# Order and queues of the first transfers, and what the warm-up multiplies, in a streamed two-block layer kernel

## The reference

```python
def first_block(x, norm1_g, w_in, ...):
    h = hybrid_layer(x, ...)
    return rmsnorm(h, final_g)

def hybrid_layer(x, layer, norm1_g, w_in, ...):
    xn = rmsnorm(x, norm1_g[layer])
    u = xn @ w_in[layer]                      # [256, 1024] @ [1024, 5632]
    q_sb, k_sb, v_sb, f_raw, i_hg, q_hg, g_hg, gate_sb, gate_hg = split(u)
    ...                                       # stick-breaking attention, HGRN2, gates, w_out
    h = x + merged @ w_out[layer]
    return h + square(relu(rmsnorm(h, norm2_g) @ w_ff1)) @ w_ff2

def second_block(x, ...):                     # two layers: gated linear attention, differential attention
    ...                                       # each followed by a SwiGLU block and a gate
```

## Time and profile before

| | us |
|---|---|
| three runs | 1041.59, 1041.59, 1043.47 (median 1041.59) |
| the profiled execution | 1042.02 |
| its span, first to last instruction | 1040.2 |

### The profile page before, as it was taken

The page is one execution under the profiler, slowest core; times in us unless marked ns, Lnnn a source line. Parts: engine busy times, 40 slices in busy tenths (PEclk is TensorE's granted clock), DMA queues, the critical chain, the costliest instruction groups (busy, mean ns, idle before and its releaser), DMA issues.

```text
span 1040.2 us, 15841 instructions
## 1 busy us (share of the span) xinstructions
PE 1033.5 (99%) x6394; PEld 911.2 (88%) x6394; DVE 729.4 (70%) x869; ACT 596.5 (57%) x752; POOL 57.4 (6%) x53
## 2 busy tenths in 40 slices
PE   8999999999999999999999999999999999999998
PEld 8998999888888889888888888889998888888887
DVE  6888887676565568965766666677989676666665
ACT  5777545553444457765644444476777664444464
POOL 0000001200000030002006000010000200000010
PEclk9999999999999999999999999999999999999999
DMA  8746353645546545355456555455524365465641
GB/s 297 235 170 199 123 200 130 214 166 196 208 162 207 198 143 202 124 184 177 162 201 209 184 186 201 163 191 174 163 82 163 132 203 202 164 207 185 211 164 41
DMA packets 129352, 185.33 MB, mean 178 GB/s; under 512 B 3328, under 2 KB 102912, under 8 KB 129280
## 3 DMA queue, kind: packets, MB, share of 16 engines
q1 hardware_dynamic: 128416, 183.27, 51.8%
q10 hardware_dynamic: 704, 0.53, 0.2%
q0 software_dynamic: 160, 0.52, 0.2%
HBM read 183.26 MB, written 1.05 MB: 177 GB/s over the span
## 4 chain that ended last, share of the span: by engine, by line
PE 97%; DVE 1%; DMA 1%; ACT 0%; issue 0%; ACTq 0%; DVEq 0%
PE PS L435 95%; PE PS L443 2%; DMA HS<-in_xt_dram 1%; DVE SC L2570 0%; DVE WL L1892 0%; ACT AR L1768 0%; DVE AR L2592 0%; ACT X L1314 0%; DVE HS L2619 0%; ACTq L426 0%; DVE O L2627 0%; DVE AR L2565 0%; DVE AR L2558 0%; ACT WH L1268 0%; ACT AR L1704 0%
## 5 line engine op out<-in xcount | busy, mean ns | idle before, releaser
L1885 DVE TENSOR_TENSOR WL<-RAW,WH 128x2048 fp32r<-128x2048 f32 (+3 forms) x174 | 371.1, 2139 | 107.1 <-ACT WH L1268 106.7
L1268 ACT ACTIVATE WH<-RAW 128x2048 fp32r<-128x2048 f32 (+3 forms) x183 | 327.8, 1794 | 80.6 <-PE PS L435 73.9
L435 PE MATMUL PS<-WH,X 128*128 128x512 f32 (+1 forms) x1104 | 302.7, 355 | 0.0
L435 PE MATMUL PS<-O,WH 128*128 128x512 f32 (+1 forms) x880 | 239.1, 361 | 0.0
L435 PEld LDWEIGHTS PS<-WH,X 128*128 128x128 f32 x1104 | 195.8, 189 | 29.8 <-issue 1.9
L435 PE MATMUL PS<-X,WH 128*128 128x256 f32 (+1 forms) x864 | 200.8, 331 | 1.9 <-ACT WH L1268 1.7
L435 PE MATMUL PS<-WL,X 128*128 128x512 f32 (+1 forms) x552 | 194.6, 353 | 0.0
L435 PEld LDWEIGHTS PS<-O,WL 128*128 128x128 f32 x744 | 134.4, 189 | 22.7
L435 PE MATMUL PS<-O,WL 128*128 128x256 f32 x744 | 153.2, 281 | 0.0
L435 PE MATMUL PS<-WH,O 128*128 128x512 f32 (+1 forms) x464 | 141.0, 378 | 0.1
L435 PEld LDWEIGHTS PS<-O,WH 128*128 128x128 f32 x880 | 137.6, 190 | 3.3 <-issue 0.3
(11 more groups left out here) (222 smaller groups left out, 778.4 us busy)
## 6 DMA issues: line engine op xcount, KB each, us to landing
RAW<-in_ffn_w_in_dram SPq DMA_DIRECT2D x44, 1024.0 KB, 5.0
RAW<-in_w_ff_dram SPq DMA_DIRECT2D x32, 1024.0 KB, 5.3
RAW<-in_ffn_w_out_dram SPq DMA_DIRECT2D x22, 1024.0 KB, 4.9
RAW<-in_w_in_dram SPq DMA_DIRECT2D x18, 1024.0 KB, 5.2
RAW<-in_gla_w_in_dram SPq DMA_DIRECT2D x12, 1024.0 KB, 5.3
RAW<-in_diff_w_in_dram SPq DMA_DIRECT2D x12, 1024.0 KB, 5.2
RAW<-in_ple_w_gate_dram SPq DMA_DIRECT2D x8, 1024.0 KB, 4.8
RAW<-in_w_out_dram SPq DMA_DIRECT2D x4, 1024.0 KB, 4.8
```

What stands on the lines that cost most here:

```text
L435: return e.matmul(o, l, r, start=start, stop=stop, skip_group_check=skip)
L1268: act(high, raw, ACT.Copy).then_inc(s["w_hi"], 1)
L1885: e.tensor_tensor(low, raw, high.bitcast(F32), ALU.subtract).then_inc(s["w_lo"], 1)
```

## The change

- ACT issues the norm weights first and then feature group 0; groups 1 and 2 are issued by SP, group 1 ahead of the joint piece of block 1, group 2 ahead of the pieces of blocks 2-3, group 3 ahead of those of blocks 4-5 as before.
- The warm-up multiplies a constant zero of the program, a tile of one column read 128 and 64 times over, that is there before the engines' programs start. It has 17 matmuls of 64 output columns instead of 7 of 128. DVE's memset and PE's wait for it go.
- ACT, which squares `HS` at line 1402, now waits for the semaphores of groups 0 and 1 itself.

```diff
-WARM = 7
+WARM = 17
+        self.zero = nc.const_aps.tensor(0.0, [128, 128])
     def warm(n):
         for _ in range(n):
-            mm(PS[:, 0, 0:128], m.ar(0, 128), m.ar(0, 128), True, True)
+            mm(PS[:, 0, 0:64], m.zero, m.zero[:, 0:64], True, True)
...
-    e.wait_ge(s["warm"], 1)
     warm(WARM)
     first_chunks()
...
+    e.dma_start(m.SML[:, 0:8], m.io["small"][:, 0:8]).then_inc(s["d_g1"], 16)
     features(e, m, 0)
-    e.dma_start(m.SML[:, 0:8], m.io["small"][:, 0:8]).then_inc(s["d_g1"], 16)
-    features(e, m, 1)
-    features(e, m, 2)
     e.preload_act_table_set(LOGEXP)
...
     for j in range(4):
         hi(w0 + 2, j)
+    for j in range(2):
+        e.wait_ge(s[f"d_x{j}"], 16)
     for j in range(2):
         act(m.ar(6528 + 1024 * j, 1024), m.HS[:, 1024 * j:1024 * j + 1024], ACT.Square).then_inc(s["row_sq"], 1)
...
-    e.memset(m.ar(0, 128), 0.0).then_inc(s["warm"], 1)
...
     for j in range(5):
+        if j in (1, 2, 3):
+            features(e, m, j)
         if j == 1:
             second_blocks()
             continue
-        if j == 3:
-            features(e, m, 3)
         piece(0, j)
         piece(1, j)
```

More of the change, by code:

```diff
@@ L202 @@
 SEMAPHORES = """raw0 raw1 raw2 part00 part01 part02 part03 part10 part12 part13 part20 part21 part22 part30 d_con d_sml d_g1 d_x0
-d_x1 d_x2 d_x3 d_h x_ss x_tot xt_first xt_hi xt_lo d_idn warm d_wg d_fg d_p d_out
+d_x1 d_x2 d_x3 d_h x_ss x_tot xt_first xt_hi xt_lo d_idn d_wg d_fg d_p d_out
 act dve pool w_hi w_lo w_lop gemm long dn rs_ms rs_y row_sq tr tr_hi tr_lo res ns_sq ns_ap rb_d rb_m rb
```

## The result

| | median us | runs |
|---|---|---|
| before | 1041.89 (1041.09 to 1044.11) | 18 |
| changed | 1043.76 (1043.32 to 1044.66) | 18 |

The ratio is 1.0015, 95% interval 1.0009 to 1.0022: 1.6 us more, at most 2.3 and at least 0.9. The forecast was 1040.8 us, 0.8 less; the median lies outside the range of 1039.4 to 1042.4, on the side of rival C. It is still inside the 0.2% that was called the same. The profiled execution took 1043.35 us with a span of 1041.5.

The account below looks back on a forecast made before the run. PE was taken to bound the kernel, its start of blocks 2-3 moving the end. The reordering's 0.84 us gain, all other parts nothing, gave 1042.02 - 0.84 = 1041.18; less 0.43 to the median, 1040.75, rounded 1040.8 us; range 1039.4 to 1042.4.

Parts of the forecast that it names:

- rival C: Warm-up too long: at 213 ns per record PE is busy until 8.4 us, blocks 2-3 start 0.7 us later; 1042.3 us, chance 0.08.
- What bounds the kernel: PE is busy 1033.5 of 1040.2 us; the start of blocks 2-3 at 10.60 us moves the end.
- Part 1, the order: New order of early transfers on SP's queue: PE starts blocks 2-3 at 9.76 us instead of 10.60, gain 0.84 us.
- f2: Transfer of feature blocks 2-3 (256 KB) at the start; forecast to land at 7.8 us, 1.15 us earlier.
- a2: Transfer of chunk 0's weight piece for blocks 2-3 (256 KB); forecast to land at 8.95 us, cast from about 9.0.
- a3: Transfer of chunk 0's weight piece for blocks 4-5 (256 KB); cast forecast at 11.91 us, limiting the gain to 0.87 us.
- Rival A: At the start, reordering gives the transfer of feature blocks 2-3 nothing: gain 0 to 0.2 us, 1041.5 us, chance 0.24.
- Rival B: Early transfers also get faster, 350 KB per us from 3 us on: gain 1.75 to 2.1 us, 1039.7 us, chance 0.17.
- B's sign of 280: Sign for Rival B: a transfer rate above 280 GB/s between 3 and 5 us.
- Part 2, the norm weights: Norm weights issued ahead of the first feature block: DVE's first block at 4.2 us as before, no gain.
- Part 3, the warm-up: PE's 34 warm-up records at 0.117 us take 4.0 us, ending near 5.1; blocks 0 and 1 done at 8.7, no cost.
- Rival D: Lighter warm-up delays PE's pace change from near 6.7 us until past 16 us: 2 us slower, chance 0.03.

## Why the prediction was wrong, step by step

**What bounds the kernel**: right in the main. In all fourteen profiles the span ends 1026.6 to 1026.9 us behind the start of blocks 4-5, whatever came before (1040.2 - 13.54 before, 1041.5 - 14.80 in the changed kernel, 1052.6 - 25.91 with forty warm-up matmuls). One premise was wrong: 6.7 us, what PE does not fill, was called the most that any change around PE is worth. PE's busy time contains the warm-up and the slow pace; the change made it 3.5 us longer with the same real work.

**Part 1, the order**: right in mechanism, and in size as far as the times tell. f2 landed at 7.6 (7.8 forecast), a2's cast began at 8.52 (9.0), a3's at 11.44 (11.91). Without the bad warm-up the gain was 0.6 us by the medians with the old one, 1.1 with nine of 128 columns, both around the 0.84 forecast. That a3 comes next as a ceiling held: blocks 4-5, forecast at 12.7, came at 12.23 with casts 0.5 us earlier than I had them, and waited for a3 until 12.55 and 12.78 in two other profiles. Rival A is out: f2 landed between 7.3 and 8.2 in all eleven profiles with the new order, between 8.6 and 9.0 in the three with the old one. The Trainium skill's turn-taking of the queues ("DMA: Bandwidth & Descriptors", section "Queues, rings and completion order"), on which that rival leaned, is not refuted by these landings, only what the rival worked out from it. Rival B did not come either: in the changed kernel the engines moved 298 GB/s at 3 to 4 us and 220 at 4 to 5, 259 over both, up from 184 but below B's sign of 280, and a2 never landed before 8.0, where B had 7.7.

**Part 2, the norm weights**: right, nothing.

**Part 3, the warm-up, is the step that failed**: it put the cost of the warm-up at nothing, and two of its terms were wrong.
First the spacing. I named both bounds, 0.117 and 0.213 us, and took 0.117 "as the row nearest in kind", though I had noted that it was "at PE's later, faster pace". Passing over that was the mistake. A load of 128 float32 columns takes 0.213 us at the slow pace and at most 0.11 us at the fast one (seventeen of 128 columns, behind the doubling), and one of 64 takes 0.107 at the slow pace; the row was from 24.95 us and the warm-up runs before 6.9. In the earlier trace rows the same PE at the slow pace had 0.213 us under 128 streamed columns, and I read that as the stream's own time, while the load took just as long beside it. So 34 x 0.213 = 7.24 us and not 4.0. (Both ends of the warm-up were also written 0.3 to 0.4 us late: 0.8 + 4.0 is 4.8 and not 5.1, 0.8 + 7.2 is 8.0 and not 8.4, and 8.02 was measured.) The Trainium skill ("TensorE: Matmul & The Clock Gate", section "LDWEIGHTS (loading the stationary operand)") gives columns / 1.2 ns, 107 ns for 128 columns, and so one figure for both paces; measured for float32 are 213 ns at the slow pace and 111 at the fast one, and the measurement decides.
Second the pace. Even rival C, which had the right spacing, let blocks 0 and 1 run in 2.9 us at the fast pace, since I took the doubling near 6.7 (it was at 6.9) as given. They took 3.9 to 4.7. With the true 8.02 in place of 8.4, C's own terms put blocks 2-3 at 10.9 and cost 0.3 us; that C gave 0.7, nearer to the truth, is luck. The slow pace adds 1.0 to 1.8: blocks 2-3 came at 11.92 to 12.74, 1.3 to 2.1 us behind the 10.60 of before. Rival D had the reason, that the lighter warm-up puts off the doubling, and was given 0.03; it was priced only for a pace low until past 16 us, and together with C a doubling at 10.2 to 12.0 was enough. C and D were not two cases but one.

Of the 3.0 us between the changed kernel and the one with nine of 128 columns (medians), the profiles show 2.75 at the start of blocks 2-3 (11.92 - 9.17) and 2.57 at that of blocks 4-5 (14.80 - 12.23), the 2.5 of the spans; the rest is the difference between executions. PE gets to real work 3.35 us later (8.02 - 4.67), of which 1.09 would have been waits for transfers anyway (0.80 + 0.29), and takes 0.49 us more for the work of blocks 0 and 1 (3.90 against 4.50 - 1.09 = 3.41).

## What to carry to other kernels

A warm-up is real work on the engine that sets the time: it has to end before the first data are there, and its length is the count of records times the longer of stream and weight load, both taken from rows at the slow pace it will run at. More and narrower matmuls behind the same full loads were not shorter here; look in the traces of several executions whether the spacing falls within the warm-up or soon behind it. Time the kernel without a warm-up too: here none at all was 2.6 us better than the wrong one and within 0.4 us of the best. Do not take the idle time of an engine as the most a change can give: a warm-up counts as busy. When two things at the start are changed together, run each alone once: here one hid the gain of the other.

## What the runs showed of the hardware that was not expected

- The profile's view of the granted clock writes 1.00 at both paces (the four windows quoted above), where 128x256 records 0.213 us apart are 256 columns at 1.2 GHz. In the traces themselves the first record of the clock, at full speed, begins just where the spacing halves: 6.9 us before, 10.2 in the changed kernel, 12.0 with the warm-up alone, 22.9 with forty of 64 columns, and likewise in the ten others. Ahead of it there is no record, and the view counts that as full. So the two agree on when the level changed, and in the view only the spacing of equal records tells it.
- PE rose to the fast pace inside the warm-up in three of the eight profiles whose warm-up streams as many columns as it loads (3.7, 3.9 and 4.1 us), and in the other five 1.3 to 4.4 us behind the end of the warm-up; with no warm-up at 9.6 us, 4.2 us into the real blocks. Behind loads of 128 columns with 64 streamed it never rose in up to 17 us of warm-up, in five profiles, but 2.2 to 5.1 us after the real blocks had begun. With the same kernel the time differs between executions: 6.9 and 5.8 us before, 10.2 and 10.6 after. How the chip decides on the level is not shown here.
- The landing of one transfer moves by over 1 us between executions of nearly the same program: a2, issued at 3.1 us in all eleven profiles with the new order, landed between 8.0 us and, in the order-alone run, 9.4. What moves it stays open; the rate of the 16 engines together does not show it.
